# The mixer's 15 head sums as two fp32r products of a split square, in place of one fp32 product each

## The reference, cut to what matters

```
h = _rmsnorm(x, g_mix); z = h @ w_in
q, k, v, mq, mk, mv, mo, ig, fg = split(z)
q = _rmsnorm(q, g_q)      # 8 heads of 64
k = _rmsnorm(k, g_k)      # 2 heads of 64
_rmsnorm(x, g) = x * rsqrt(mean(x*x, -1) + 1e-6) * g
```

## Time and profile before

| | us |
|---|---|
| median of 3 runs | 1971.97 |
| the profiled execution's own time | 1972.91 |
| its span | 1971.3 |
| TensorE busy | 1943.2 (99%) |
| VectorE busy | 1304.7 (66%) |
| GpSimd busy | 1068.0 (54%) |
| ScalarE busy | 778.3 (39%) |
| the stage, TensorE's units 1 to 20 | about 744.7 to 840.9 |
| of it in the fp32 head sums, 30 records | 7.8 + 3.9 |

### The profile page before, as it was taken

One profiled execution on the slowest core, in us unless ns is written; L12 is line 12 of the kernel. 1 busy time (PEld: TensorE's weight loads), 2 busy tenths in 40 slices (PEclk: granted clock), 3 DMA queues, 4 the chain that ended last, 5 costly groups with the idle time before them and its releaser, 6 DMA issues.

```text
span 1971.3 us, 39251 instructions
## 1 busy us (share of the span) xinstructions
PE 1943.2 (99%) x14645; PEld 1899.2 (96%) x14645; DVE 1304.7 (66%) x1882; ACT 778.3 (39%) x1585; POOL 1068.0 (54%) x960
## 2 busy tenths in 40 slices
PE   7999999999999999999999999999999999999998
PEld 7999999999999999989998999999999999999997
DVE  7766777667566788754445664867777677657674
ACT  6433333333443344733434542343333333344343
POOL 2277776775777651231222442237776777586760
PEclk9999999999999999999999999999999999999999
DMA  8135445334986530342331744214354345498552
GB/s 267 45 111 172 143 158 179 130 130 154 312 306 188 174 92 15 100 126 84 93 97 62 201 115 122 77 41 157 131 175 162 130 133 180 132 359 280 172 155 102
DMA packets 226846, 293.88 MB, mean 149 GB/s; under 512 B 16616, under 2 KB 158472, under 8 KB 226736
## 3 DMA queue, kind: packets, MB, share of 16 engines
q1 hardware_dynamic: 219040, 272.76, 43.0%
q0 software_dynamic: 7696, 19.63, 3.2%
HBM read 198.07 MB, written 94.21 MB: 148 GB/s over the span
## 4 chain that ended last, share of the span: by engine, by line
PE 90%; DVE 3%; DMA 2%; ACT 2%; POOL 1%; issue 1%; SPq 1%; DVEq 0%; ACTq 0%; POOLq 0%
PE bank L281 28%; PE bank L283 28%; PE bank L282 28%; PE bank L2521 1%; PE bank L2540 1%; PE bank L2531 1%; DMA RAWU<-in_w_up 1%; DMA WRAW<-in_w_down 1%; DVE RSC L2134 1%; SPq L1544 0%; PE bank L2630 0%; PE bank L1313 0%; PE bank L1311 0%; PE bank L1312 0%; PE bank L2622 0%
## 5 line engine op out<-in xcount | busy, mean ns | idle before, releaser
L283 PE MATMUL bank<-HA,HW 128*128 128x272 f32 x1120 | 322.8, 288 | 0.0
L281 PE MATMUL bank<-HA,HW 128*128 128x272 f32 x1120 | 322.5, 288 | 0.3 <-DVE HW L1360 0.3
L282 PE MATMUL bank<-HA,HW 128*128 128x272 f32 x1120 | 321.6, 287 | 0.0
L1360 DVE SCALAR_TENSOR_TENSOR HW<-WRAW,HW 128x512 fp32r<-128x512 f32 x140 | 225.2, 1647 | 104.4 <-ACT HW L1355 104.1
L1366 POOL TENSOR_TENSOR HA<-ARAW,HA 128x544 fp32r<-128x544 f32 x140 | 220.4, 1591 | 104.8 <-ACT HA L1354 104.6
L281 PE MATMUL bank<-HH,WGH 128*128 128x362 f32 (+2 forms) x808 | 264.2, 327 | 2.9 <-DVE HL L343 2.9
L283 PE MATMUL bank<-HH,WGL 128*128 128x362 f32 (+2 forms) x808 | 254.7, 315 | 1.5 <-issue 1.5
L282 PE MATMUL bank<-HL,WGH 128*128 128x362 f32 (+2 forms) x808 | 254.8, 315 | 0.0
L281 PE MATMUL bank<-FC,WR 128*128 128x272 f32 x768 | 222.1, 289 | 0.3 <-issue 0.2
L283 PE MATMUL bank<-FC,WR 128*128 128x272 f32 x768 | 221.7, 289 | 0.0
L282 PE MATMUL bank<-FC,WR 128*128 128x272 f32 x768 | 221.1, 288 | 0.0
(11 more groups left out here) (370 smaller groups left out, 5681.9 us busy)
## 6 DMA issues: line engine op xcount, KB each, us to landing
asp<-SA SPq DMA_DIRECT2D x44, 544.0 KB, 3.4
RAWG<-in_w_gate SPq DMA_DIRECT2D x22, 1024.0 KB, 6.4
RAWU<-in_w_up SPq DMA_DIRECT2D x22, 1024.0 KB, 6.4
tsp<-TT SPq DMA_DIRECT2D x40, 544.0 KB, 6.4
ARAW<-tsp SPq DMA_DIRECT2D x80, 272.0 KB, 3.4
WS<-in_w_down SPq DMA_DIRECT2D x20, 1024.0 KB, 8.6
wsp<-WS SPq DMA_DIRECT2D x20, 1024.0 KB, 8.5
WRAW<-wsp SPq DMA_DIRECT2D x80, 256.0 KB, 4.4
```

Source lines behind the costliest of these rows:

```text
L281: nc.tensor.matmul(bank[:, 0:w], w_hi, rhs_hi, start=first, stop=False)
L282: nc.tensor.matmul(bank[:, 0:w], w_hi, rhs_lo, start=False, stop=False)
L283: return nc.tensor.matmul(bank[:, 0:w], w_lo, rhs_hi, start=False, stop=last)
L1360: nc.vector.scalar_tensor_tensor(out=HW[f][h][:, 1], in0=WRAW[r][:, :], scalar=0.5, in1=HW[f][h][:, 0].bitcast(F32), op0=ALU.mult, op1=ALU ...
```

## The change

The squares are split. ScalarE still squares the bank into SQC. After the copy into ZST or KTT it now also copies SQC into SQX with type fp32r, which rounds it (the high part), and GpSimd subtracts SQX from SQC into SQL, in SQC's place (the low part). TensorE then makes two fp32r matmuls, BD by SQX and BD by SQL, into the same bank, and waits for the low part (z.slo) rather than for the square. BD is fp32r: it is built in DT0 and copied by one more GpSimd instruction near the program's start. The semaphore z.sqc now counts two per unit.

On GpSimd the queue has a new order: for i = 0 to 15, first the low part of i (if i is under 15), then the store of normed unit i - 2 up to i = 8, of i - 2 and i - 1 at i = 9, and of i - 1 from then on, each with all that stands behind it. The rest is bookkeeping (64 bytes more for SQX, FS placed over SSB, a semaphore less).

```diff
-                nc.tensor.matmul(BANK[HEAD_BANK[i]][:, 0:w], BD[:, :], squares_of(i), start=True, stop=True).then_inc(z.bd, 1)
+                nc.tensor.matmul(BANK[HEAD_BANK[i]][:, 0:w], BD[:, :], squares_of(i, SQX), start=True, stop=False)
+                nc.tensor.matmul(BANK[HEAD_BANK[i]][:, 0:w], BD[:, :], squares_of(i, SQL), start=False, stop=True).then_inc(z.bd, 1)
...
-                pe.wait_ge(z.sqc, i + 1)
+                pe.wait_ge(z.slo, i + 1)
...
                     nc.scalar.activation(normed_out(c), bank[:, 0:w], ACT.Copy, scale=GQ[:, 1:2] if j == 3 else GQ[:, 0:1]).then_inc(z.zg, 1)
+                    act.wait_ge(z.sqc, 2 * i + 1)
+                    nc.scalar.activation(squares_of(i, SQX), squares_of(i, SQC), ACT.Copy).then_inc(z.sqc, 1)
                 if c - 1 in NORMED:
                     normed_root(NORMED.index(c - 1))
...
-            for q, c in enumerate(STORED):
+            def low_squares(i):
+                pool.wait_ge(z.sqc, 2 * i + 2)
+                nc.gpsimd.tensor_tensor(squares_of(i, SQL), squares_of(i, SQC), squares_of(i, SQX).bitcast(F32), ALU.subtract).then_inc(z.slo, 1)
+
+            def store_normed(q, c):
...
+            for i in range(len(NORMED) + 1):
+                if i < len(NORMED):
+                    low_squares(i)
+                for k in [i - 2] if i < 9 else [i - 2, i - 1] if i == 9 else [i - 1]:
+                    if k >= 0 and NORMED[k] in STORED:
+                        store_normed(STORED.index(NORMED[k]), NORMED[k])
...
+            nc.gpsimd.tensor_copy(BD[:, :], DT0[:, 0:P]).then_inc(const_ops, 1)
```

More of the change, by code:

```diff
@@ L85, in build @@
         rD = region("d", 3 * 8192)
-        rT = region("t", 8 * NW * 4)
+        rT = region("t", 8 * NW * 4 + 64)
         rC = region("c", 0)
@@ L144, in build @@
         SQC = [place(f"SQC{i}", [P, NW], F32, (rT + 4 * NW * 4, rD + 8704)[i]) for i in range(2)]
+        SQL = [place(f"SQL{i}", [P, NW], F32R, (rT + 4 * NW * 4, rD + 8704)[i]) for i in range(2)]
+        SQX = [place(f"SQX{i}", [P, NW], F32R, (rT + 4 * NW * 4, rD + 8704)[i] + 3 * 1472) for i in range(2)]
         RSC = [[place(f"RSC{i}{k}", [P, NW], F32, (rT + 4 * NW * 4, rD + 8704)[i] + (1 + k) * 1472) for k in range(2)] for i in range(2)]
@@ L147, in build @@
         KTOK = place("KTOK", [P, 2, P], F32, rD + 10240 + (NB + 1) * 512)
-        assert 8704 + 3 * 1472 <= 16384 and 3 * 1472 <= 4 * NW * 4 and 10240 + (NB + 3) * 512 <= 3 * 8192 - 2 * T * 4
+        assert 8704 + 4 * 1472 <= 16384 and 4 * 1472 <= 4 * NW * 4 + 64 and 10240 + (NB + 3) * 512 <= 3 * 8192 - 2 * T * 4
         QB = place("QB", [P, 2, 4, P], F32, rD)
@@ L181, in build @@
         ONES = place("ONES", [P, P], F32, rC + 512)
-        BD = place("BD", [P, P], F32, rC + 1024)
+        BD = place("BD", [P, P], F32R, rC + 1024)
         DT = place("DT", [P, 2 * P], F32, rC + 1536)
@@ L210, in build @@
         DEN = small("DEN", [4])
-        FS = small("FS", [4, 4])
         DECAY = small("DECAY", [2, LH])
         DENB = small("DENB", [NB + 1, LH])
+        FS = place("FS", [P, 4, 4], F32, small_at)
         SSB = small("SSB", [NB + 1, LH])
@@ L245, in build @@
         block_in = x_in + zin + [sem("block_in7"), sem("block_in8")]
-        z = named("z", "padded hi lo mm ev sqc bd rsc zg rc scaled")
+        z = named("z", "padded hi lo mm ev sqc slo bd rsc zg rc scaled")
         zst = [sem(f"zst{s}") for s in range(4)]
         g = named("g", "f ab e ln lf b m r u ws col colev out")
-        vk = named("vk", "tr ev out kout cin ctr cev pad")
+        vk = named("vk", "tr ev out kout cin cev pad")
         at_in = [sem("at_in0"), sem("at_in1")]
@@ L265, in build @@
         down_hi, HI_FROM = dist_abs, 1
-        down_alo, ALO_FROM = const_ops, 15
+        down_alo, ALO_FROM = const_ops, 16
         down_t_out, T_FROM = block_in[8], 16
@@ L1524, in build, with squares_of @@
         LAST_SUM = [max([k for k in range(i) if HEAD_BANK[k] == HEAD_BANK[i]], default=None) for i in range(len(NORMED))]
-        def squares_of(i):
-            return SQC[NORMED[i] < 12][:, 0:NTILE[M1[NORMED[i]][1]][1]]
+        def squares_of(i, tiles):
+            return tiles[NORMED[i] < 12][:, 0:NTILE[M1[NORMED[i]][1]][1]]
         def roots_of(i):
@@ L1644, in _ @@
             nc.gpsimd.memset(ONES[:, :], 1.0).then_inc(const_ops, 1)
-            nc.gpsimd.memset(BD[:, :], 0.0).then_inc(const_ops, 1)
+            nc.gpsimd.memset(DT0[:, 0:P], 0.0).then_inc(const_ops, 1)
             nc.gpsimd.memset(MC[:, :], 0.0).then_inc(const_ops, 1)
@@ L1656, in _ @@
             pool.wait_ge(const_ops, 9)
-            nc.gpsimd.memset(BD[0:HD, 0:HD], 1.0).then_inc(const_ops, 1)
+            nc.gpsimd.memset(DT0[0:HD, 0:HD], 1.0).then_inc(const_ops, 1)
             pool.wait_ge(const_ops, 10)
-            nc.gpsimd.memset(BD[HD:P, HD:P], 1.0).then_inc(const_ops, 1)
+            nc.gpsimd.memset(DT0[HD:P, HD:P], 1.0).then_inc(const_ops, 1)
             pool.wait_ge(const_ops, 11)
             pool.wait_ge(dist_abs, 1)
+            nc.gpsimd.tensor_copy(BD[:, :], DT0[:, 0:P]).then_inc(const_ops, 1)
             nc.gpsimd.memset(DT[0:HD, 3 * HD:4 * HD], MASKED).then_inc(const_ops, 1)
-            pool.wait_ge(const_ops, 12)
+            pool.wait_ge(const_ops, 13)
             nc.gpsimd.memset(DT[HD:P, 0:HD], MASKED).then_inc(const_ops, 1)
-            pool.wait_ge(const_ops, 13)
+            pool.wait_ge(const_ops, 14)
             nc.gpsimd.tensor_copy(DT0[:, P:2 * P], DT[:, P:2 * P]).then_inc(const_ops, 1)
@@ L1885, in _ @@
                     wait_done(act, z.bd, i)
-                    nc.scalar.activation(squares_of(i), bank[:, 0:w], ACT.Square).then_inc(z.sqc, 1)
+                    nc.scalar.activation(squares_of(i, SQC), bank[:, 0:w], ACT.Square).then_inc(z.sqc, 1)
                     if j >= 4 and STORED.index(c) >= 4:
@@ L1966, in one_head @@
                     if first and t == 1:
-                        act.wait_ge(vk.ctr, 1)
+                        act.wait_ge(vk.tr, 4)
                         nc.scalar.activation(CKT[:, :], BANK[7][:, 0:P], ACT.Copy).then_inc(vk.cev, 1)
@@ L2230, in att_low @@
                 nc.vector.tensor_tensor(HL[:, 0:4, t0:t0 + w], ATT[:, :, t0:t0 + w], HH[:, 0:4, t0:t0 + w].bitcast(F32), ALU.subtract).then_inc(att_lo, 1)
-            dve.wait_ge(const_ops, 15)
+            dve.wait_ge(const_ops, 16)
             one_head(0, first=True)
@@ L2491, in _ @@
                 else:
-                    pe.wait_ge(z.sqc, NORMED.index(c - 4) + 1)
+                    pe.wait_ge(z.sqc, 2 * NORMED.index(c - 4) + 1)
                     pe.wait_ge(z.zg, NORMED.index(c - 4) + 1)
@@ L2509, in _ @@
             pe.wait_ge(z.zg, len(NORMED))
-            pe.wait_ge(z.sqc, len(NORMED))
+            pe.wait_ge(z.sqc, 2 * len(NORMED))
             pe.wait_ge(vk.ev, 3)
@@ L2563, in one_head @@
                         pe.wait_ge(vk.cin, 16)
-                        nc.tensor.transpose(BANK[7][:, 0:P], CKV[:, :], IDENT[:, :]).then_inc(vk.ctr, 1)
+                        nc.tensor.transpose(BANK[7][:, 0:P], CKV[:, :], IDENT[:, :]).then_inc(vk.tr, 1)
             one_head(0, first=True)
```

## The result

The changed kernel takes 1977.74 us in the median of 10 runs (1974.44 to 1980.43); the kernel before, in 10 runs of its own beside them, 1971.09 (1967.0 to 1973.5). The medians lie 6.6 us apart; the ratio of the runs is 1.0029, 95% interval 1.002 to 1.0037, which is 5.7 us (3.9 to 7.3). So the change makes the kernel slower, where +4.7 us was forecast. The profiled execution took 1977.38 us, with a span of 1975.8 and a granted clock of 0.994.

What follows compares the result with a forecast made beforehand. Behind 784 us ScalarE, VectorE and GpSimd were taken to bound the stage, not TensorE. Softmax delay +6.2, clock -3.4 and +1.2, collisions +0.7 gave +4.7 us: 1976.7 us median, range 1971.5 to 1984.

Steps and rivals of the forecast that it cites:

- What bounds the stage: From 784 us to the softmax, ScalarE, VectorE and GpSimd are late; TensorE has spare time and waits 2.6 us before the transposes.
- TensorE's 0.28 us per sum, 1.1 us of it counting: Two fp32r products save 0.28 us per head sum, 4.2 in all; only i = 0 to 3 bring the end forward.
- The subtraction at 1.05 us: GpSimd's subtraction of 362 columns for each low part takes 1.05 us, bounds 0.96 and 2.28.
- The 0.1 for each signal: Each signal between engines, before and after the subtraction, adds 0.1 us before a head sum can start.
- The stall at i = 4, 1.9: TensorE stalls 1.9 us before the sum of i = 4, where ScalarE is behind with the gates' Exp and Ln.
- The stalls behind the stores: Low parts queue behind GpSimd's stores and DMA issues: stalls of 3.3, 1.85, 1.5, 1.7 and 1.35 us at i = 10 to 14.
- The collisions, +0.7, put on the five late low parts: GpSimd's subtraction and VectorE's two-input operations share a port: 0.1 to 0.2 us for each of five late low parts, +0.7.
- The clock: Half clock leaves the transposes (wait 1.4 us), -3.4; it comes behind the 3.3 us stall at i = 10, +1.2 left.
- The sum: The whole kernel is 4.7 us slower, 1976.7 us in the median; own range +2.5 to +8.
- no change: Rival: GpSimd's DMA issues do not hold its subtraction, only ScalarE's lateness stalls; +0.6, 1972.6 us; chance 0.22.
- Faster: Rival: the 1.1 us gained before 784 us stay and the half clock at the transposes goes; 1967.5 us; chance 0.06.
- Much slower: Rival: the clock stays at its lower level across the five stalls, +12 more, 1989 us; chance 0.12.

Runs made afterwards that it cites:

- pe_only: The kernel before with one fp32r product per head sum, low part left out, nothing added on ScalarE or GpSimd: 1969.17 us, ratio 0.9992.
- first_four: The changed kernel with the split for i = 0 to 3 alone, the other sums by one fp32 product: 1969.36 us, ratio 0.9992.
- tiny_low: The changed kernel with GpSimd's subtraction cut to 4 columns from 362, second product taking the high part again: 1971.47 us, ratio 1.0003.
- split_sp: The changed kernel with the stage's later DMAs issued by SyncE and GpSimd storing unit i - 2 to the end: 1974.28 us, ratio 1.0013.
- skip_scans: The changed kernel with the fp32 product back for i = 6 to 9 alone: 1974.63 us, ratio 1.001.
- before_sp: The kernel before with the stage's later DMAs issued by SyncE, nothing else changed: 1970.34 us, ratio 0.9995.
- last_five: The changed kernel with the split for i = 10 to 14 alone, the other sums by one fp32 product: 1976.55 us, ratio 1.0028.
- split_copy: The changed kernel without GpSimd's subtraction; ScalarE's copy stays and the second product takes the high part again: 1969.11 us, ratio 0.9987.
- split_sp_soft: The kernel before with later DMAs on SyncE, VectorE's first softmax ahead of the last reciprocal and scaling, plus the whole split: 1970.27 us, ratio 0.9992.

## Why the prediction was right, step by step

- **What bounds the stage.** Right. With nothing added (pe_only) 6.7 us less of products moved the transposes by 2.5, and the wait there grew.
- **TensorE's 0.28 us per sum, 1.1 us of it counting.** Right: 4.61 became 4.33, and first_four's profile moved by 1.4.
- **The subtraction at 1.05 us.** Right alone: 0.98 in the median. Not in the worst, 2.49, above the upper bound of 2.28. The 0.1 for each signal, for which the prediction shows no row, was 0.05 to 0.1: the copy of i = 4 ended at 789.79 and its subtraction began at 789.87, that one ended at 790.81 and the sum began at 790.87.
- **The stall at i = 4, 1.9.** Right: 1.74.
- **The stalls behind the stores.** The mechanism is right (tiny_low and split_sp: shorten or free the queue and they shrink); the sizes are not. At i = 10, 4.2 and not 3.3: the store left at 821.80, which by the mark of the stage's start is 2.7 later than in before, where 0.6 was reckoned; the 2.1 between is the three longer VectorE operations. TensorE arrived 1 us later than drawn too, 0.4 of it in a wait at i = 9 that I did not have and the rest in steps of 0.1 or 0.2. At i = 13, 2.6 and not 1.7, and the sum itself, by the mark at 845.85, is 3.1 us later than drawn. The store ahead of it accounts for 2.5 of these: it left 5.0 later than in before, not 2.5, since ScalarE's square of i = 11 waits for the sum of i = 10, and through it the delay of that sum went into ScalarE's gate work, the root of i = 11 and its reciprocal. The rest is the low part of 1.73 us beside a weight rounding of VectorE (1.97). The stalls at i = 11, 12 and 14 were 0, 0.3 and 0, since half clock had already delayed TensorE. In all it waited 9.3 us for low parts, where 11.6 were forecast.
- **The collisions, +0.7, put on the five late low parts.** This is the term that was mis-sized, and misplaced: 2.1 us fell on VectorE beside the low parts of i = 6 to 9, which I had called in time and therefore free. They were in time for TensorE; it was the other engine that paid. The trace of before had the sign of it, beside the very row that the prediction quotes from the earlier trace rows (line 324 is a sum and not a subtraction, but it has two inputs too). VectorE's line 343 takes 1.66 us in five of its six places and 2.83 where it began while GpSimd's line 322 ran:

```profile
737.26 1.66 DVE L343 TENSOR_TENSOR HL<-SQa,HH 128x1456 fp32r<-128x1456 f32 x1
739.28 1.75 POOL L322 TENSOR_TENSOR SQH<-SQH 128x724 f32<-128x724 f32 x1 [4.92 <-ACT SQH L297]
739.73 2.83 DVE L343 TENSOR_TENSOR HL<-SQb,HH 128x1456 fp32r<-128x1456 f32 x1
```

- **The clock.** Right in part, and in part luck. The half clock left the transposes, where 1.4 us of wait was forecast and 1.3 came, and appeared behind i = 10. It was worth 2.9 us at the transposes by the marks, not 3.4. The second one, behind i = 13, was not foreseen. The 1.2 us that the forecast lets through, by way of ScalarE's square of i = 12, did not come that way: this square, at 831.05, followed ScalarE's own work with no wait. And the two rows that the forecast goes by, 2.6 us answered and 1.7 not, don't make a rule: skip_scans has half clock after 1.6 us, before_sp none after 2.3.
- **The sum.** +4.7 forecast, +5.7 measured. In the stage the miss is larger: the softmax is 10.5 us late and not 6.2, and the first product of weights and values 7.6, after 2.9 of half clock given back, where the forecast has +4.7. The profiled execution ends only 4.5 later than before's, since its stage began 1.8 earlier and it was 1.3 faster behind that product, neither of which the forecast is about. So the direction and the mechanism were forecast, and that the final number came within 1 us is in part luck. The errors lie on one side, and the own range of +2.5 to +8 held them.

Of the rivals, no change needed stores that do not hold: they do. Faster needed a softmax no later than before: it was 10.5 later. Much slower needed the lower clock across all five stalls: the full clock came back at 829.3 and stayed up to the wait at i = 13, and three of the five stalls shrank or went.

Left open: how the 5.7 us divide between queue, length and collisions, since they feed one another (without the three long collisions, skip_scans, the loss is 2.0; without most of the queue, split_sp, 2.6; without length, tiny_low, none to be measured). last_five lacks those collisions too and still loses 5.5 by its ratio, though at the first product it is 1.4 us ahead of skip_scans; nothing in the stage explains why its time is the longer of the two.

## What to carry to other kernels

Read the chain in order of time around the edit, not its shares: an engine with 90% of a chain can still be the waiting one through the stage in which the change lies, and a shorter matmul then buys mostly a longer wait. Work moved to an engine that issues DMAs is priced by what stands ahead of it in that engine's queue and by what the stores there wait for, and an operation that is in time for its reader can still lengthen the two-operand operations of VectorE beside it. Before giving work away from the waiting engine, look for an instruction on the late one that its next reader does not need; here moving one reciprocal and one scaling, with the DMAs on SyncE, was worth 5 us, some 4 of them by the move itself.

## What the hardware showed beyond what was expected

- VectorE pays for a neighbour on GpSimd even on four partitions and 64 columns: 0.32 became 0.99 us. A copy on ScalarE at the same places (split_copy) lengthened none of the three.
- A wait of TensorE was followed by half clock after 4.6, 4.2, 4.1, 3.4, 2.6 (in before and in after), 2.3 (first_four, and i = 10 of tiny_low), 1.9 (i = 10 of skip_scans and of split_sp_soft) and 1.6 us (i = 13 of skip_scans); in last_five it came behind a wait of 0.46 at i = 13, the fourth in 20 us. It did not follow 2.3 us in before_sp, 1.9 at i = 10 of split_sp, or 2.0 and 1.8 in last_five. So in these traces the length of the wait alone does not tell. Each of them made the next step or stretch 1.5 to 2.9 us longer.
- Half clock inside a stage whose later steps stall anyway can cost nothing: behind i = 10 of after it made the step 2.75 us longer than 4.33. The low part of i = 11 ended at 828.18, so at full clock (an estimate from these rows) TensorE would have waited 0.5 us there, and 2.6 in place of 0.3 at i = 12, whose low part, held by the queue, ended at 835.14 in any case. Behind i = 13 it did cost: the low part of i = 14 ended at 849.71, and the sum began at 851.06.
